# Encoder trunk: the first loads split into six transfers, x prepared by token tile, rstd ahead of the mask's cast, and branch B's mask added on VectorE in the row maximum

## The chip, the cores and the metric

One core of a Trainium2 chip runs the whole program. The metric is the time on the device in microseconds (us), lower is better. The kernel before took 861.21 us (median of 3 runs, 860.22 to 861.93). Engines are named as in the profile: PE (TensorE), DVE (VectorE), ACT (ScalarE), POOL (GpSimd), SP (SyncE).

## The reference

Two layers of an encoder on x of shape (1, 256, 1024), float32:

```
h  = rmsnorm(x);  z = h @ W_in            # columns: A q|k|v, B q|k|v, C pool, gates
A  = grouped-query attention, 8 heads, all 256 keys
B  = dilated windows, 3 groups x 4 slots: sc = where(valid, q.k / 8, -1e30)
     m = max(sc); p = exp(sc - m); groups joined by their softmax denominators
C  = centred mean pooling (windows 2/4/8/16) minus the token, a linear map
x += (sum_i sigmoid(gate_i) * P_i(branch_i)) @ W_out
x += SwiGLU(rmsnorm(x))
```

## The kernel before

All weights come as one stream of 136 units (68 for each layer) of 1 MB, each a tile of 128 partitions x 4 x 512 float32. SP loads them into a ring of four buffers, `w_raw` (L382 to L388); a buffer is loaded again when PE is done with its unit. Every float32 value is split into two float32r parts. ACT writes the high part (`w_hi`, L484, and for a layer's first unit in four quarters, L480), DVE subtracts to get the low part (`w_lo`, L621 and L627). The activations are split alike (`aT_hi` at L494, `aT_lo` at L654). PE then makes three matmuls of 512 columns for each product: hi x hi (L881), hi x lo (L883), lo x hi (L892). A unit has two token tiles m of 8 + 4 matmuls each.

The order is written by hand and is the same for all engines: for each unit t there is "before" work (`turns_before`), scores of attention pairs (units 11, 13, ..., 25), their transposes one unit later and the product with the values two units later, the unit's matmuls, and "within" work (`turns_within`). Each engine runs this list in order; semaphores tie them.

The start. `x_sb` holds x, tokens in two tiles. Half 0 of its columns (512 KB) is loaded by SP, half 1 by POOL. PE transposes four 128x128 blocks of it for each pair of half and tile (`("mix_x", i)`: i = 0, 1 are half 0 with tiles 0 and 1; i = 2, 3 are half 1), DVE multiplies by the norm's gain (L645), ACT makes the high part, DVE the low part. In unit 0, ACT splits the unit's four quarters, then units 1 and 2, and only then makes the high parts of mix_x 2 and 3; then it squares x with a sum (L530), and POOL makes rstd from the sums (L426, L420, L422). rstd is needed when ACT moves chunk z0 out of PSUM (L587, L588) in unit 1. POOL copies the identity and the mask to bfloat16 (L446, L448) before it makes rstd. DVE makes the rotary tables in unit 1 and from unit 2 on it rotates q and k (L693 to L717), between the low parts of the weights.

Attention. For each of 16 score tiles of 128x512 (two form a pair) PE writes scores to PSUM, DVE takes the row maximum with its sign changed (L731), ACT the exponential with a row sum (L516 to L523), DVE scales by the reciprocal of the sum (L742, L746), PE transposes (L914), ACT copies (L506). Tiles 8 to 15 are branch B. There the mask is added by PE: a bfloat16 matmul of the identity with the mask (L994) opens the accumulation and the scores (L1000) add to it.

Of the kernel before, what the change touches and what calls it, by code (L numbers as in the profile page):

```python
# [18 lines left out]
BF16 = mybir.dt.bfloat16  # L19
# [4 lines left out]
P = 128  # L24
# [3 lines left out]
NEG_INF = -1e30  # L28
MT = SEQ // P
KT = D // P  # L30
NC = 512
# [12 lines left out]
FIRST_BYTE, SMALL_BYTES = 4224, 11168  # L44
# [151 lines left out]
EARLY_TURNS = 2  # L196
BEFORE = -1
# [11 lines left out]
def build(nc, x, stream, params, b_gate, eye, angles, pooling, mask, out):  # L209
# [3 lines left out]
    with ExitStack() as ctx:  # L213
# [18 lines left out]
        mask_sb = sb("mask_sb", [P, P + MT * NC], BF16)  # L232
# [43 lines left out]
        ident_b = mask_sb[:, 0:P]  # L276
        mask_m = [mask_sb[:, P + m * NC:P + (m + 1) * NC] for m in range(MT)]
# [5 lines left out]
        x0_loaded = sem("x0_loaded")  # L283
# [5 lines left out]
        mask_ready = sem("mask_ready")  # L289
        gains_loaded = sem("gains_loaded")  # L290
        params_loaded = sem("params_loaded")
        bias_loaded = [sem(f"bias_loaded{i}") for i in range(2)]
        unit_landed = [sem(f"unit_landed{i}") for i in range(RING)]
        unit_done = sem("unit_done")
# [14 lines left out]
        max_ready = sem("max_ready")  # L309
        probs_ready = sem("probs_ready")  # L310
# [67 lines left out]
        @block.sync  # L378
        def _(sp):
            sp.dma_start(x_sb[:, :, 0:NC], xv[:, :, 0:NC]).then_inc(x0_loaded, 16)  # L380
            sp.dma_start(ident[:, :], eye).then_inc(eye_loaded, 16)
            with sp.Fori(0, DEPTH * UNITS // RING) as turn:  # L382
                for s in range(RING):

                    sp.wait_ge(unit_done, turn * RING + (s + 1))
                    sp.dma_start(w_raw[:, s, :, :].rearrange("p k n -> p (k n)"),  # L386
                                 stream_v[bass.ds((turn * RING + s) * P, P), :]
                                 ).then_inc(unit_landed[s], 16)  # L388

            ov = out.rearrange("b (p m) d -> (b p) m d", m=MT)  # L390
            for half, first in enumerate(X_BANKS):
                for m in range(MT):
                    sp.wait_ge(bank_free[first + m], DEPTH * USES[first + m] + 1)
                    cols = slice(NC * half, NC * half + NC)
                    sp.dma_start(ov[:, m, cols], x_sb[:, m, cols]).then_inc(out_done, 16)
            sp.wait_ge(out_done, 16 * 2 * MT)

        @block.gpsimd
        def _(pool):
# [9 lines left out]
            load_gains(0)  # L409
            pool.dma_start(x_sb[:, :, NC:D], xv[:, :, NC:D]).then_inc(x1_loaded, 16)  # L410
# [29 lines left out]
            for lay in range(DEPTH):  # L440
                load_bias(lay, 0)
                load_bias(lay, 1)
                if lay == 0:

                    pool.wait_ge(eye_loaded, 16)
                    nc.gpsimd.tensor_copy(mask_sb[:, 0:P], ident[:, :]).then_inc(mask_ready, 1)  # L446
                    pool.wait_ge(mask_loaded, 16)
                    nc.gpsimd.tensor_copy(mask_sb[:, P:], mask_f).then_inc(mask_ready, 1)  # L448
                x_norms(lay, 0, 0)
                if lay == 0:  # L450
                    pool.dma_start(pool_mat[:, :, :, :].rearrange("p m g n -> p (m g n)"), pooling
                                   ).then_inc(pooling_loaded, 16)
# [12 lines left out]
                x_norms(lay, 1, 2 + TURNED)  # L465

                wait_lo(pool, lay, ("ffn_x", 3))
                load_gains(min(lay + 1, DEPTH - 1))
                load_params(min(lay + 1, DEPTH - 1))

        @block.scalar
        def _(act):
            for b in range(0, 8):
                act.sem_inc(bank_free[b], 1)

            def split_first(lay):

                act.wait_ge(unit_landed[0], lay * (16 * UNITS // RING) + 16)
                for k in range(UK):
                    nc.scalar.activation(w_hi[:, 0, k, :], w_raw[:, 0, k, :], ACT.Copy).then_inc(first_hi, 1)  # L480
# [30 lines left out]
            def softmax_exp(lay, i):  # L511

                act.wait_ge(max_ready, lay * ATT + (i + 1))
                if i < 8:
                    m, h = i // 4, 4 * (i % 2) + 2 * (i // 2 % 2)
# [5 lines left out]
                else:  # L521
                    m, s = (i - 8) // 4, i % 4
                    last = nc.scalar.activation(probs[:, i % 2, :], B(("s", i))[:, :], ACT.Exp,  # L523
                                                bias=neg_max[:, 2 * i:2 * i + 1],
                                                accum_out=den[:, m, 8 + s:9 + s])
# [10 lines left out]
            act.wait_ge(x0_loaded, 16)  # L536
            for i in range(EARLY_TURNS):
                turn(BEFORE, ("mix_x", i))
            for lay in range(DEPTH):
                for t in range(UNITS):  # L540
                    for name in turns_before(t):
                        turn(lay, name)
                    if t == 0:
                        split_first(lay)
                    for j in splits_at(t, ahead=3):
                        split(lay, j)
# [11 lines left out]
                    for name in turns_within(t):  # L558
                        turn(lay, name)
# [9 lines left out]
                    if t % 2 == 1 and t // 2 <= POOL_CHUNK:  # L569
# [3 lines left out]
                        if c == 4:  # L573
                            act.wait_ge(mask_ready, 2)
# [31 lines left out]
        def _(dve):  # L606
# [121 lines left out]
            def row_max(lay, i):  # L728
                wait_full(dve, lay, ("s", i))
                k = 2 if i < 8 else 1  # L730
                nc.vector.tensor_reduce(neg_max[:, 2 * i:2 * i + k],  # L731
                                        B(("s", i))[:, :].rearrange("p (h n) -> p h n", h=k), AX_X, ALU.max,
                                        negate=True).then_inc(max_ready, 1)

            def norm_probs(lay, i):
# [5 lines left out]
                wait_emptied(dve, lay, ("s", i))  # L741
# [46 lines left out]
            dve.wait_ge(gains_loaded, 16)  # L788
            turns(BEFORE, [("mix_x", i) for i in range(EARLY_TURNS)])
            for lay in range(DEPTH):  # L790
# [3 lines left out]
                for t in range(UNITS):  # L794
# [4 lines left out]
                    if t == U_DOWN + 7:  # L799
                        dve.wait_ge(gains_loaded, lay * 16 + 32)  # L800
                    turns(lay, turns_before(t))
                    if t == 0:
                        split_first(lay)
                    if t in TURNS_FIRST:
                        turns(lay, turns_within(t))
# [60 lines left out]
        def _(pe):  # L866
            pe.sem_inc(unit_done, RING)

            def rows(lay, t, name, m, src, tiles, wk, first, final, opening=False):
# [4 lines left out]
                if first:  # L874
                    wait_free(pe, lay, (name, m))
                if opening and t:
# [21 lines left out]
            def columns(lay, t, name, src, tiles, first, final, wk=0):  # L898

                rows(lay, t, name, 0, src, tiles, wk, first, final, opening=wk == 0)  # L900
# [3 lines left out]
                return rows(lay, t, name, 1, src, tiles, wk, first, final)  # L904
# [66 lines left out]
            def scores(lay, p):  # L971
# [7 lines left out]
                if p == 4:  # L979
                    pe.wait_ge(mask_ready, 2)  # L980
# [11 lines left out]
                else:  # L992
                    for r in range(2):
                        nc.tensor.matmul(banks[r][:, :], ident_b, mask_m[m], start=True, stop=False)  # L994
                    for g in range(GROUPS):
# [3 lines left out]
                        for r in range(2):  # L999
                            last[r] = nc.tensor.matmul(banks[r][:, cols], qkT[rows_of[r], QT_B_Q + tile, tok],  # L1000
                                                       qkT[rows_of[r], QT_B_K + tile, keys], start=False,
                                                       stop=(g == GROUPS - 1))
# [29 lines left out]
            pe.wait_ge(x0_loaded, 16)  # L1032
            pe.wait_ge(eye_loaded, 16)
            for i in range(EARLY_TURNS):
                transposes(BEFORE, ("mix_x", i))
            for lay in range(DEPTH):
                for t in range(UNITS):
# [6 lines left out]
                    if t < U_C0:  # L1044
                        c, half = divmod(t, 2)
                        if c == 0:
                            for m in range(MT):
                                wait_lo(pe, lay, ("mix_x", 2 * half + m), former=half == 0)
                        last = columns(lay, t, f"z{c}", aT, range(UK * half, UK * half + UK), half == 0, half == 1)
# [15 lines left out]
                    elif t < U_FFN:  # L1065
                        half, n = divmod(t - U_OUT, 2)
                        if n == 0:
                            for m in range(MT):
                                wait_emptied(pe, lay, ("merged", 2 * half + m))
                        last = columns(lay, t, f"W{n}", aT, range(UK * half, UK * half + UK), half == 0, half == 1)  # L1070
                    elif t < U_DOWN:
                        i, half = divmod(t - U_FFN, 2)
                        if i == 0:
                            for m in range(MT):
                                wait_lo(pe, lay, ("ffn_x", 2 * half + m))
                        last = columns(lay, t, f"f{i}", aT, range(UK * half, UK * half + UK), half == 0, half == 1)
# [119 lines left out]
```

## Time and profile before

| what | value |
|---|---|
| the profiled execution's own time | 861.18 us |
| its span | 859.4 us |
| PE busy | 842.9 us, 98% |
| DVE busy | 552.0 us, 64% |
| ACT busy | 419.6 us, 49% |
| POOL busy | 74.1 us, 9% |

The span is what the profile covers; 1.8 us of the execution lie outside it. Busy shares are averages over stages. A pair of a time and a duration such as "11.69 0.77" is the start of a group of instructions and how long it lasted. "idle before" names how long the engine did nothing and what released it.

### The profile page before, as it was taken

Reading aid. Unit: us, or ns where it says so; the run is one execution under the profiler, and the core shown is the slowest. Engines: PE = TensorE matmul, PEld = TensorE weight load, DVE = VectorE, ACT = ScalarE, POOL = GpSimd, SP = SyncE. Lnnn points to the kernel's source line nnn. Section 1 sums busy time; section 2 is a strip of 40 time slices with the busy share of each in tenths; the row PEclk is TensorE's granted clock in tenths of the full one; section 3 lists DMA queues with packets and bytes.
Section 4 is the critical chain, followed back from the end, with each engine's and each line's share of the span. In section 5 each row is a group of like instructions: output and inputs, shape, how many; then the busy total and the mean of one; then the engine's idle time right before and its main releaser. Section 6 shows DMA issues by size and latency. Waiting matters only on the chain.

```text
span 859.4 us, 10421 instructions
## 1 busy us (share of the span) xinstructions
PE 842.9 (98%) x4060; PEld 687.1 (80%) x4068; DVE 552.0 (64%) x672; ACT 419.6 (49%) x505; POOL 74.1 (9%) x89
## 2 busy tenths in 40 slices
PE   4999999999999999999999999999999999999998
PEld 3788777878888888888888877878788888888886
DVE  3799556565876656564468985556576766566552
ACT  4665654455453444443446575443834544444340
POOL 2343000000002000000022420000000200000000
PEclk9999999999999999999999999999999999999999
DMA  8555434444547555555545543433454555555551
GB/s 327 210 183 195 147 117 154 172 147 148 191 153 240 195 176 174 189 196 195 180 170 194 191 153 142 170 131 141 148 196 170 193 195 186 170 185 192 196 184 61
DMA packets 22427, 151.59 MB, mean 176 GB/s; under 512 B 2624, under 2 KB 2800, under 8 KB 4848
## 3 DMA queue, kind: packets, MB, share of 16 engines
q1 hardware_dynamic: 20576, 144.25, 47.4%
q0 software_dynamic: 1808, 6.72, 2.3%
q8 instruction: 32, 0.52, 0.2%
q14 instruction: 11, 0.09, 0.0%
HBM read 149.91 MB, written 1.05 MB: 176 GB/s over the span
## 4 chain that ended last, share of the span: by engine, by line
PE 97%; DMA 2%; issue 0%; ACT 0%; SPq 0%; DVE 0%; ACTq 0%
PE bank L881 29%; PE bank L883 29%; PE bank L892 29%; PE bank L914 5%; PE bank L1025 2%; DMA w_raw<-in_stream_dram 2%; PE bank L1000 1%; PE bank L989 1%; PE bank L961 1%; PE bank L967 0%; PE bank L994 0%; ACT zvu L588 0%; DVE aT_lo L654 0%; ACT probsT L506 0%; SPq L386 0%
## 5 line engine op out<-in xcount | busy, mean ns | idle before, releaser
L621 DVE TENSOR_TENSOR w_lo<-w_raw,w_hi 128x2048 fp32r<-128x2048 f32 x134 | 306.3, 2288 | 130.9 <-ACT w_hi L484 130.6
L881 PE MATMUL bank<-w_hi,aT_hi 128*128 128x512 f32 x832 | 334.3, 402 | 6.8 <-ACT w_hi L480 4.9
L883 PE MATMUL bank<-w_hi,aT_lo 128*128 128x512 f32 x832 | 326.5, 392 | 0.0
L484 ACT ACTIVATE w_hi<-w_raw 128x2048 fp32r<-128x2048 f32 x134 | 256.3, 1913 | 106.1 <-DMA w_raw<-in_stream_dram 106.0
L892 PE MATMUL bank<-w_lo,aT_hi 128*128 128x512 f32 x832 | 224.2, 391 | 0.0
L881 PEld LDWEIGHTS bank<-w_hi,aT_hi 128*128 128x128 f32 x832 | 157.1, 189 | 43.4 <-issue 9.7
L892 PEld LDWEIGHTS bank<-w_lo,aT_hi 128*128 128x128 f32 x832 | 156.3, 188 | 33.2 <-DVE w_lo L627 0.2
L883 PEld LDWEIGHTS bank<-w_hi,aT_lo 128*128 128x128 f32 x832 | 157.3, 189 | 31.0
L881 PE MATMUL bank<-w_hi,hT_hi 128*128 128x512 f32 x176 | 68.9, 391 | 0.0
L883 PE MATMUL bank<-w_hi,hT_lo 128*128 128x512 f32 x176 | 68.5, 389 | 0.0
L499 ACT ACTIVATE hT_hi<-bank 128x512 fp32r<-128x512 f32 x22 | 13.2, 598 | 78.3 <-PE bank L914 78.3
L602 ACT ACTIVATE sg<-bank,rstd 128x256 f32<-128x256 f32 x44 | 20.9, 475 | 58.2 <-PE bank L892 51.8
L892 PE MATMUL bank<-w_lo,hT_hi 128*128 128x512 f32 x176 | 47.7, 389 | 0.0
L657 DVE TENSOR_TENSOR hT_lo<-bank,hT_hi 128x512 fp32r<-128x512 f32 x22 | 15.2, 692 | 41.1 <-ACT hT_hi L499 41.1
L731 DVE TENSOR_REDUCE neg_max<-bank 128x2 f32<-128x512 f32 (+1 forms) x32 | 20.6, 685 | 29.4 <-PE bank L1000 16.8
L506 ACT ACTIVATE probsT<-bank 128x512 f32<-128x512 f32 x32 | 17.5, 595 | 44.4 <-PE bank L914 44.2
L892 PEld LDWEIGHTS bank<-w_lo,hT_hi 128*128 128x128 f32 x176 | 33.0, 188 | 6.9
L881 PEld LDWEIGHTS bank<-w_hi,hT_hi 128*128 128x128 f32 x176 | 33.0, 188 | 6.8
L883 PEld LDWEIGHTS bank<-w_hi,hT_lo 128*128 128x128 f32 x176 | 33.1, 188 | 6.7
L426 POOL TENSOR_TENSOR sx<-ssx 128x2 f32<-128x2 f32 x4 | 4.3, 1080 | 361.5 <-ACT probsT L530 361.5
L850 DVE SCALAR_TENSOR_TENSOR scratch<-bank,rstd,sg 128x256 f32<-128x256 f32 x44 | 21.1, 481 | 21.2 <-ACT sg L602 21.2
L422 POOL TENSOR_TENSOR rs<-rs_in,neg_half 128x8 f32<-128x8 f32 (+2 forms) x24 | 32.8, 1365 | 2.0
(97 smaller groups left out, 704.0 us busy)
## 6 DMA issues: line engine op xcount, KB each, us to landing
w_raw<-in_stream_dram SPq DMA_DIRECT2D x136, 1024.0 KB, 4.7
bias_sb<-in_b_gate_dram POOLq DMA_DIRECT2D x12, 256.0 KB, 4.5
par<-in_params_dram POOLq DMA_DIRECT2D x3, 384.0 KB, 4.3
pool_mat<-in_pooling_dram POOLq DMA_DIRECT2D x1, 1024.0 KB, 8.3
out_dram<-x_sb SPq DMA_DIRECT2D x4, 256.0 KB, 4.0
x_sb<-in_x_dram SPq DMA_DIRECT2D x1, 512.0 KB, 3.7
x_sb<-in_x_dram POOLq DMA_DIRECT2D x1, 512.0 KB, 8.2
gates<-in_mask_dram POOLq DMA_DIRECT2D x1, 512.0 KB, 14.4
```

The lines of the kernel that those rows point to most:

```text
L422: nc.gpsimd.tensor_tensor(dst[0], dst[1], dst[2], ALU.pow).then_inc(signal, 1)
L484: nc.scalar.activation(w_hi[:, j % RING, :, :].rearrange("p k n -> p (k n)"), w_raw[:, j % RING, :, :].rearrange("p k n -> p (k n)"), ACT. ...
L506: free(nc.scalar.activation(probsT[:, i % 2, :], B(name)[:, :], ACT.Copy), name)
L602: nc.scalar.activation(sg[:, i % 2, m, :], B((f"f{i}", m))[:, 0:256], ACT.Sigmoid, scale=rstd[:, 1, m:m + 1]).then_inc(sig_done, 1)
L621: nc.vector.tensor_tensor(w[0], w[1], w[2].bitcast(F32), ALU.subtract).then_inc(unit_lo, 1)
L731: nc.vector.tensor_reduce(neg_max[:, 2 * i:2 * i + k], B(("s", i))[:, :].rearrange("p (h n) -> p h n", h=k), AX_X, ALU.max, negate=True).t ...
L850: made.append(link(nc.vector.scalar_tensor_tensor(scratch[:, 2 * NC + 256 * m:2 * NC + 256 * m + 256], B((f"f{i}", m))[:, 0:256], rstd[:, ...
L881: nc.tensor.matmul(o, src[0][:, k, tok], w_hi[:, slot, wk + i, :], start=first and i == 0, stop=False)
L883: nc.tensor.matmul(o, src[1][:, k, tok], w_hi[:, slot, wk + i, :], start=False, stop=False)
L892: last = nc.tensor.matmul(o, src[0][:, k, tok], w_lo[:, slot, wk + i, :], start=False, stop=final and i == len(tiles) - 1)
L914: return nc.tensor.transpose(b[:, at:at + P], src, ident[:, :])
L1025: last = nc.tensor.matmul(B(("o", o))[HD * r:HD * r + HD, at:at + w], zvu[:, kt, col(r):col(r) + HD], probsT[:, r, c:c + cw], start=(n == ...
```

## The change

- SP issues, before its loop: x half 0 tile 0, quarter 0 of unit 0, x half 0 tile 1, quarters 1 to 3 of unit 0 (six transfers of 256 KB), then x half 1 (512 KB, from POOL's queue to SP's), then units 1 to 3. The loop starts at the second turn.
- ACT issues the identity (from SP's queue) and the first layer's gains (from POOL's queue). POOL waits for x half 1 before it issues parameters, angles, mask and bias.
- PE runs 14 tiny matmuls on a constant tile once that tile is set, and 10 more after the transposes of mix_x 0 and 1.
- ACT and DVE prepare mix_x 1 after the quarters of unit 0; in layer 0 ACT makes the high parts of mix_x 2 and 3 ahead of the splits of units 1 and 2. PE waits for each token tile's low part by itself, also at W_out and the SwiGLU's first chunk.
- POOL makes rstd before it waits for the mask and casts it. There is no bfloat16 identity any more.
- Branch B: no mask matmuls. DVE's row maximum is one `tensor_tensor_reduce` that adds the mask, changes the sign, writes 128x512 to SBUF and keeps the row minimum; it frees the PSUM bank. ACT's exponential reads and writes that SBUF tile.

```diff
@@ SP
-            sp.dma_start(x_sb[:, :, 0:NC], xv[:, :, 0:NC]).then_inc(x0_loaded, 16)
-            sp.dma_start(ident[:, :], eye).then_inc(eye_loaded, 16)
-            with sp.Fori(0, DEPTH * UNITS // RING) as turn:
+            def first_piece(k):
+                sp.dma_start(w_raw[:, 0, k, :], stream_v[0:P, NC * k:NC * k + NC]).then_inc(piece_landed[k], 16)
+            sp.dma_start(x_sb[:, 0, 0:NC], xv[:, 0, 0:NC]).then_inc(x0_loaded[0], 16)
+            first_piece(0)
+            sp.dma_start(x_sb[:, 1, 0:NC], xv[:, 1, 0:NC]).then_inc(x0_loaded[1], 16)
+            for k in range(1, UK):
+                first_piece(k)
+            sp.sem_inc(unit_landed[0], 16)
+            sp.dma_start(x_sb[:, :, NC:D], xv[:, :, NC:D]).then_inc(x1_loaded, 16)
+            for s in range(1, RING):
+                sp.dma_start(w_raw[:, s, :, :].rearrange("p k n -> p (k n)"), stream_v[s * P:s * P + P, :]
+                             ).then_inc(unit_landed[s], 16)
+            with sp.Fori(1, DEPTH * UNITS // RING) as turn:
@@ POOL
-            load_gains(0)
-            pool.dma_start(x_sb[:, :, NC:D], xv[:, :, NC:D]).then_inc(x1_loaded, 16)
+            pool.wait_ge(x1_loaded, 16)
             load_params(0)
...
-                if lay == 0:
-                    pool.wait_ge(eye_loaded, 16)
-                    nc.gpsimd.tensor_copy(mask_sb[:, 0:P], ident[:, :]).then_inc(mask_ready, 1)
-                    pool.wait_ge(mask_loaded, 16)
-                    nc.gpsimd.tensor_copy(mask_sb[:, P:], mask_f).then_inc(mask_ready, 1)
                 x_norms(lay, 0, 0)
                 if lay == 0:
+                    pool.wait_ge(mask_loaded, 16)
+                    nc.gpsimd.tensor_copy(mask_sb[:, :], mask_f).then_inc(mask_ready, 1)
@@ ACT
+            act.dma_start(ident[:, :], eye).then_inc(eye_loaded, 16)
+            act.dma_start(par[:, 0:PR_GAIN], params_v[0:P, 0:PR_GAIN]).then_inc(first_gains, 16)
...
+                    wait_emptied(act, lay, ("s", i))
+                    nc.scalar.activation(probs[:, i % 2, :], probs[:, i % 2, :], ACT.Exp, scale=-1.0,
+                                         bias=neg_max[:, 2 * i:2 * i + 1],
+                                         accum_out=den[:, m, 8 + s:9 + s]).then_inc(exp_done, 1)
...
                     if t == 0:
                         split_first(lay)
+                        if lay == 0:
+                            turn(BEFORE, ("mix_x", 1))
+                            for name in turns_within(t):
+                                turn(lay, name)
                     for j in splits_at(t, ahead=3):
                         split(lay, j)
@@ DVE
+                    free(nc.vector.tensor_tensor_reduce(probs[:, i % 2, :], B(("s", i))[:, :], mask_m[(i - 8) // 4],
+                                                        -1.0, BIG, ALU.add, ALU.min, neg_max[:, 2 * i:2 * i + 1]),
+                         ("s", i))
...
-            turns(BEFORE, [("mix_x", i) for i in range(EARLY_TURNS)])
+            scale_turn(BEFORE, ("mix_x", 0))
+            scale_turn(BEFORE, ("mix_x", 1))
+            low_turn(BEFORE, ("mix_x", 0))
@@ PE
-                    for r in range(2):
-                        nc.tensor.matmul(banks[r][:, :], ident_b, mask_m[m], start=True, stop=False)
...
+            def warm_up(n):
+                for _ in range(n):
+                    nc.tensor.matmul(bank[WARM_BANK][0:MT * HEADS, 0:MT * HEADS],
+                                     neg_half[:, :, :].rearrange("p m h -> p (m h)"),
+                                     neg_half[:, :, :].rearrange("p m h -> p (m h)"), start=True, stop=True)
+            pe.wait_ge(half_ready, 1)
+            warm_up(WARM_LOADS)
             pe.wait_ge(eye_loaded, 16)
             for i in range(EARLY_TURNS):
+                pe.wait_ge(x0_loaded[i], 16)
                 transposes(BEFORE, ("mix_x", i))
+            warm_up(WARM_SPLITS)
```

## Rows read from the trace of the kernel before

**Rows 1.** The page's first part: busy time, share, instructions of each engine.
```profile
PE 842.9 (98%) x4060; PEld 687.1 (80%) x4068; DVE 552.0 (64%) x672; ACT 419.6 (49%) x505; POOL 74.1 (9%) x89
```
**Rows 2.** Waits of PE: who waited for whom, us in total, times, longest.
```profile
PE bank L881 <- ACT w_hi L480: 4.9, 1, 4.9
PE bank L881 <- DVE aT_lo L654: 1.9, 1, 1.9
```
**Rows 3.** Timeline of the first 30 us: start, duration, instructions merged, idle before.
```profile
4.85 1.94 PE L914 MATMUL bank<-ident,x_sb 128*128 128x128 f32 x8 [4.85 <-DMA ident<-in_eye_dram]
6.05 1.47 DVE L645 TENSOR_TENSOR scratch<-bank,par 128x512 f32<-128x512 f32 x2 [6.05 <-PE bank L914]
10.92 2.19 ACT L480 ACTIVATE w_hi<-w_raw 128x512 fp32r<-128x512 f32 x4 [2.74 <-DMA w_raw<-in_stream_dram]
14.73 1.91 ACT L484 ACTIVATE w_hi<-w_raw 128x2048 fp32r<-128x2048 f32 x1 [1.62 <-DMA w_raw<-in_stream_dram]
21.27 0.61 ACT L530 ACTIVATE probs<-x_sb 128x512 f32<-128x512 f32 x1
23.90 0.52 POOL L426 TENSOR_TENSOR sx<-ssx 128x2 f32<-128x2 f32 x1 [4.61 <-ACT probsT L530]
26.70 2.65 POOL L422 TENSOR_TENSOR rstd<-sx,neg_half 128x2 f32<-128x2 f32 x1
28.52 1.07 PE L892 MATMUL bank<-w_lo,aT_hi 128*128 128x512 f32 x4
```
**Rows 4.** DMA issues of the first 12 us: KB each, median us to landing.
```profile
x_sb<-in_x_dram SPq DMA_DIRECT2D x1, 512.0 KB, 3.7
gates<-in_mask_dram POOLq DMA_DIRECT2D x1, 512.0 KB, 14.4
```
**Rows 5.** Two windows: busy us of PE, PEld, DVE, ACT, POOL, PE's clock, DMA share, GB/s.
```profile
23.08:26.49 3.41, 3.41 (x10) 2.66 (x9) 3.41 (x3) 2.53 (x5) 2.50 (x2) 0.52 0.48 199
40.20:88.10 47.90, 47.78 (x224) 38.70 (x222) 47.15 (x77) 30.85 (x47) 16.48 (x20) 1.00 0.50 176
```
**Rows 6.** Timeline rows of DVE and PE, 33 to 89 us.
```profile
33.65 2.29 DVE L621 TENSOR_TENSOR w_lo<-w_raw,w_hi 128x2048 fp32r<-128x2048 f32 x1 [2.99 <-ACT w_hi L484]
...
40.20 2.29 DVE L621 TENSOR_TENSOR w_lo<-w_raw,w_hi 128x2048 fp32r<-128x2048 f32 x1 [1.54 <-ACT w_hi L484]
...
86.43 1.07 PE L892 MATMUL bank<-w_lo,aT_hi 128*128 128x512 f32 x4
...
87.57 0.62 DVE L746 TENSOR_SCALAR probs<-probs,rden 128x256 f32<-128x256 f32 x2
...
88.31 0.42 PEld L914 LDWEIGHTS bank<-ident,probs 128*128 128x128 f32 x4 [0.31 <-issue]
```
**Rows 7.** PE's timeline where the scores of branch A, then branch B, begin.
```profile
79.22 1.08 PE L892 MATMUL bank<-w_lo,aT_hi 128*128 128x512 f32 x4
...
80.22 1.14 PE L989 MATMUL bank<-qkT 64*128 64x256 f32 x8
...
157.11 1.08 PE L892 MATMUL bank<-w_lo,aT_hi 128*128 128x512 f32 x4
...
158.56 1.15 PE L1000 MATMUL bank<-qkT 64*128 64x256 f32 x12
```
**Rows 8.** DVE's operations by line, then timeline rows of pair 5.
```profile
L731 DVE TENSOR_REDUCE neg_max<-bank 128x2 f32<-128x512 f32 (+1 forms) x32 | 20.6, 685 | 29.4 <-PE bank L1000 16.8
L621 DVE TENSOR_TENSOR w_lo<-w_raw,w_hi 128x2048 fp32r<-128x2048 f32 x134 | 306.3, 2288 | 130.9 <-ACT w_hi L484 130.6
...
L833 DVE SCALAR_TENSOR_TENSOR gates<-bank,rstd,bias_sb x24: 739/748/751, 116.5 to 615.6; 128x512 f32<-128x512 f32 x24
...
163.93 0.49 DVE L746 TENSOR_SCALAR probs<-probs,rden 128x512 f32<-128x512 f32 x1
...
166.06 1.02 PEld L914 LDWEIGHTS bank<-ident,probs 128*128 128x128 f32 x8
```

More of the change, by code:

```diff
@@ L27 @@
 EPS = 1e-6
-NEG_INF = -1e30
+NEG_INF, BIG = -1e30, 3e38
 MT = SEQ // P
@@ L293, in build @@
         unit_landed = [sem(f"unit_landed{i}") for i in range(RING)]
+        piece_landed = [sem(f"piece_landed{k}") for k in range(UK)]
         unit_done = sem("unit_done")
@@ L535, in _ @@
             nc.scalar.activation(table_warm[:, :], neg_half[:, 0, 0:MT], ACT.Exp)
-            act.wait_ge(x0_loaded, 16)
-            for i in range(EARLY_TURNS):
-                turn(BEFORE, ("mix_x", i))
+            for m in range(MT):
+                act.wait_ge(x0_loaded[m], 16)
+            turn(BEFORE, ("mix_x", 0))
             for lay in range(DEPTH):
@@ L867, in _, with rows @@
             pe.sem_inc(unit_done, RING)
-            def rows(lay, t, name, m, src, tiles, wk, first, final, opening=False):
+            def rows(lay, t, name, m, src, tiles, wk, first, final, opening=False, ready=None):
                 tok = slice(P * m, P * m + P)
@@ L896, in rows, with columns @@
                 return last
-            def columns(lay, t, name, src, tiles, first, final, wk=0):
-                rows(lay, t, name, 0, src, tiles, wk, first, final, opening=wk == 0)
+            def columns(lay, t, name, src, tiles, first, final, wk=0, ready=None):
+                rows(lay, t, name, 0, src, tiles, wk, first, final, wk == 0, ready)
                 if wk == 0 and t not in TURNS_FIRST:
@@ L903, in columns @@
                         transposes(lay, turn)
-                return rows(lay, t, name, 1, src, tiles, wk, first, final)
+                return rows(lay, t, name, 1, src, tiles, wk, first, final, False, ready)
             def transposes(lay, name):
@@ L1045, in _ @@
                         c, half = divmod(t, 2)
[L1046 to L1049, printed above, removed]
+                        ready = (lambda m: wait_lo(pe, lay, ("mix_x", 2 * half + m), former=half == 0)) if c == 0 else None
+                        last = columns(lay, t, f"z{c}", aT, range(UK * half, UK * half + UK), half == 0, half == 1,
+                                       ready=ready)
                     elif t in (U_C0, U_C1):
@@ L1066, in _ @@
                         half, n = divmod(t - U_OUT, 2)
[L1067 to L1070, printed above, removed]
+                        ready = (lambda m: wait_emptied(pe, lay, ("merged", 2 * half + m))) if n == 0 else None
+                        last = columns(lay, t, f"W{n}", aT, range(UK * half, UK * half + UK), half == 0, half == 1,
+                                       ready=ready)
                     elif t < U_DOWN:
                         i, half = divmod(t - U_FFN, 2)
[L1073 to L1076, printed above, removed]
+                        ready = (lambda m: wait_lo(pe, lay, ("ffn_x", 2 * half + m))) if i == 0 else None
+                        last = columns(lay, t, f"f{i}", aT, range(UK * half, UK * half + UK), half == 0, half == 1,
+                                       ready=ready)
                     else:
```

57 lines of the change are left out of this document (33 added, 24 removed).

## The prediction

> **What bounds the kernel now.** I read the page's busy shares first. PE is busy 842.9 of 859.4 us [rows 1], so only PE's idle time, its work and its clock can be worth anything. PE's waits come next: beside the first loads they hold one wait of 4.9 us before its first matmul of unit 0 and one of 1.9 us before unit 1 [rows 2]. Together with the first transposes at 4.85 us [rows 3] all of the idle time lies in the first 23 us. The timeline of that stretch shows who is late: ACT's split of unit 0 waits for the DMA until 10.92, its split of unit 1 until 14.73 [rows 3]. PE ends unit 1 at 28.52 + 4 x 0.227 = 29.43 us (0.227 us is the pitch of these matmuls: four take 1.07, which is three pitches and one duration of 0.39). That 29.43 is my reference point at the start.
>
> Then I looked at windows for an engine that is full beside PE. From 40.20 to 88.10 us DVE is busy 47.15 of 47.90 us [rows 5]: rotations between weight splits. At its end PE has its last matmul of unit 11 at 86.43 (done at 87.34), DVE normalizes the first pair's probabilities at 87.57 (done 88.1), and PE's second group of their weight loads starts at 88.31, right behind [rows 6]. So in layer 0 PE and DVE reach unit 12 together, and PE already waits about 0.3 us there. Whoever starts PE earlier must start DVE earlier too.
>
> **The change part by part.**
>
> *First loads.* x's half 0 (512 KB) landed 3.7 us after its issue at 0.73 [rows 4], at 4.4. Half of it first in the queue lands at about 3.8 (256 KB at about 400 GB/s is 0.65 us). Tile 1 is third, 512 KB behind, so about 5.2; the quarters follow 0.65 us apart up to 7.2, x half 1 at 8.6, unit 1 at 11.3, unit 2 at 14 to 15, unit 3 at 17 to 19, since POOL's loads join at about 10. I take 4.1 for the identity, which PE had to wait for until 4.85 [rows 3] as second in SP's queue.
>
> *First matmul.* PE transposes tile 0 at 4.1 and tile 1 at 5.2 (8 took 1.94, so 4 take 0.9 to 1.0); the first scaling started 1.2 us behind the transposes' start and takes 0.73 [rows 3], so DVE scales tile 0 at 5.3 and tile 1 at 6.4 to 7.1, and makes the low part of tile 0 by 7.8. ACT has quarter 0 ready by 7.1, and all four by 8.8 (0.55 each, rows 3). The first matmul is at 7.8 instead of 11.69 = 3.9 us earlier. The 14 tiny matmuls lie before 4.1 and the 10 before 7.8: I cost them at nothing; if each took 0.2 us the ten would end at 8.0 and cost 0.2.
>
> *Unit 0 and 1.* DVE makes the four low quarters by 10.4, the low part of tile 1 by 11.1, then scales mix_x 2 and 3; ACT's high parts of them are done by 13.1 if PE runs unit 0 at the high clock, by 14.5 if at the low one. ACT splits unit 1 by 15.1 (1.91 us, rows 3), DVE's low part is there at 17.3, PE ends unit 1 at about 20.9 (16 hi matmuls, two short waits). PE would be 8.5 us ahead; with the low clock in unit 0, 7.1 us. The 1.9 us wait [rows 2] is inside this, its cause (ACT made mix_x 2 and 3 behind the split of unit 2) is gone.
>
> *rstd.* ACT: split of unit 1 to 15.1, unit 2 to 17.0, squares from 17.1; squares to POOL's first step took 23.90 - 21.27 = 2.6 us, POOL's three steps 26.70 + 2.65 - 23.90 = 5.45 us [rows 3]. rstd is ready at 25.2 instead of 29.35: 4.15 us earlier, less than PE's 8.5. The mask's cast is 1 us on POOL that did not stand in the way before (POOL waited 4.61 us for the squares, rows 3), so its move is worth 0; but POOL now meets the mask's wait behind rstd. The mask took 14.4 us to land [rows 4]; issued at about 10 it is there by 24.4, before rstd: 0. In the worst case, with all of POOL's loads 5 us later, POOL's first head norms (needed 7 us behind rstd) still don't wait.
>
> *DVE.* Its split of unit 4 began 33.65 - 29.35 = 4.3 us behind rstd, since ACT moves z0 first; it idled 1.54 us before the split of unit 5 [rows 6], whose load ran beside the 1 MB pooling matrix. Now unit 5's load starts at about 21, well ahead of that matrix: this idle time should go. DVE reaches the first pair's probabilities 4.15 + 1.54 = 5.7 us earlier, at 82.4 instead of 88.1. Bounds: 4.15 (idle time stays) less 1.3 (low clock in unit 0, late landing) = 2.9, and 8.8 (no gate: 8.5 and the 0.3 of waiting). I take 5.7, since the stretch behind it is full work.
>
> *PE at unit 12.* PE is ready at 87.34 - 8.5 = 78.8 and DVE at 81.7 for the first tile: a new wait of about 2.9 us (1.5 with the low clock in unit 0). After the one wait of this size (1.9 us) the granted clock stood at 0.52, the lower level of 1.2 GHz, from 23.08 to 26.49 [rows 5], costing half of 3.41 = 1.7 us. I count that again here.
>
> *Mask matmuls.* From the last low matmuls' start to the scores' start branch B has 158.56 - 157.11 = 1.45 us, branch A 80.22 - 79.22 = 1.00 us [rows 7]. 0.45 us for each of 4 pairs in 2 layers: 3.6 us of PE's time, all on the path.
>
> *The new row maximum.* The trace has no such operation. Nearest rows: a reduction from PSUM of the same shape 0.685 us, a three-operand op from PSUM 0.748, and, far off, 2.29 for four times the elements [rows 8]. I take 0.75, with ends 0.68 and 2.29. Pair 5 shows the room: DVE is done at 163.93 + 0.49 = 164.42, PE reads at 166.06 [rows 8], 1.64 us of slack, and two such operations at 0.75 take 0.13 more than now. Even double passes (1.37 each) stay inside. The exponential now reads SBUF; ACT is idle half of the time. So 0. The Trainium skill ("VectorE: DVE Perf Modes", section on two Vector instructions with no wait between them) says that an operation with an accumulator output is two instructions. No row of DVE here shows a second one; by that rule both tiles of a pair get a bit longer, inside the slack.
>
> The Trainium skill ("DMA: Bandwidth & Descriptors", rules for kernel authors) holds that spreading DMAs over engines brings no bandwidth, as all share the same 16 DMA engines. By it moving loads between SP, ACT and POOL is worth only what their order is worth, and that is how I cost them.
>
> *PE's waits by token tile* at W_out and the SwiGLU: PE has no wait there now (none in rows 2), so 0.
>
> Sum, against the profiled execution: 861.2 (861.18, span 859.4; the median is 861.21, so nothing to correct) - 5.7 + 1.7 - 3.6 = 853.6 us.
>
> **The rivals.**
>
> *The clock stays up at unit 12.* The wait may be split in two by the first tile's transposes, or shorter. For it: 1.5 us if PE is slower in unit 0. Against it: the only precedent fell. Time: 853.6 - 1.7 = 851.9.
>
> *DVE is no gate.* DVE's lag behind PE would have to be made up. For it: ACT and the loads run ahead, PE's lead is real. Against it: 47.15 of 47.90. Time: 861.2 - 8.8 - 3.6 = 848.8.
>
> *The start is later than I think.* 256 KB transfers of 2 KB rows, POOL's loads in front of unit 2, PE at the low clock in unit 0: rstd moves by only 2.9 us. With a short wait at unit 12 that keeps the clock, or a long one: 861.2 - 2.9 - 3.6 (+ 1.7) = 854.7 to 856.4.
>
> *Slower.* The new DVE operation is slow, as when it makes several passes over a PSUM source. Each pair then holds PE by 2(x - 0.685) - 1.64 = 2x - 3.0 us, eight times. It decides at 7.6 = 8(2x - 3.0), x = 1.98 us. At 2.29 [rows 8] it gives 8 x 1.6 = 12.6 us: 866.2. For it: the operation is not in the trace. Against it: both near rows lie at 0.7.
>
> *The change does not do what it says.* PE's first data could be held by something that I don't see, for instance ACT's issue of DMAs before its table load; then only the mask's 3.6 us are left with part of the start, 857.
>
> **How the numbers follow.** Forecast 0.43 (853.6); clock stays 0.25 (851.9); later start 0.15 (855.5); no gate 0.08 (848.8); little at the start 0.04 (857.3); slower 0.05 (866). A measurement of this kernel tells 0.2%, 1.7 us, from no change. Faster: all but the last and a little of the one before, 0.94; same 0.02; slower 0.04. The range leaves out "no gate", the slow case and some of the edges: 850.3 to 857.0.
>
> **What would show it.** First L881 matmul at about 7.8 us; rstd's L422 ends near 25; the 1.9 us wait for aT_lo is gone; DVE full from about 34 to 82; a PE wait of 1.5 to 3 us at L914 near 79 to 82 us, followed by a stretch of clock 0.5; L1000 starts 1.00 us after the last L892 row; the new DVE operation near 0.75 us and no wait of PE for probabilities of branch B. I am wrong if PE passes unit 12 without a wait, if the new operation is over 1.5 us, or if unit 2 starts later than 24 us.

## The result and the profile after

The changed kernel takes 849.45 us (median of 4 runs, 848.44 to 850.21) beside 861.43 us of the kernel before in the same comparison: ratio 0.9865 (95% interval 0.9851 to 0.988), 10.3 to 12.8 us less. I had forecast 853.6 us with a range of 850.3 to 857.0. The direction was right, the size wrong: the start gave about twice what I had put down for it.

The spans of the two profiled executions differ by 859.4 - 847.9 = 11.5 us. First the page's busy shares and PE's waits (us in total, times, longest) of the changed kernel:

```profile
PE 842.3 (99%) x4100; PEld 689.4 (81%) x4100; DVE 552.7 (65%) x688; ACT 420.1 (50%) x505; POOL 69.2 (8%) x86
```
```profile
PE bank L1067 <- POOL neg_half L422: 0.9, 1, 0.9
PE bank L950 <- ACT probsT L521: 0.8, 2, 0.4
PE bank L950 <- DMA ident<-in_eye_dram: 0.3, 1, 0.3
PE bank L950 <- DMA x_sb<-in_x_dram: 0.2, 1, 0.2
```

Both waits of [rows 2] are gone, and no new one of any size has come; PE's 5.9 us of tiny matmuls (L1067; each of the 24 stands as two records, so x28 and x20 below) count as busy here, so the busy time hardly falls although 3.6 us of mask work are gone.

The timeline of the start (line numbers have moved: L667 was L645, L495 was L480, L917 was L881, L928 was L892, L547 was L530, L439, L433 and L435 were L426, L420 and L422):

```profile
4.64 1.12 PE L950 MATMUL bank<-ident,x_sb 128*128 128x128 f32 x4 [0.26 <-DMA ident<-in_eye_dram]
5.92 1.12 PE L950 MATMUL bank<-ident,x_sb 128*128 128x128 f32 x4 [0.16 <-DMA x_sb<-in_x_dram]
...
6.82 2.48 PE L1067 MATMUL bank<-neg_half 128*68 128x68 f32 x20
...
7.21 2.18 ACT L495 ACTIVATE w_hi<-w_raw 128x512 fp32r<-128x512 f32 x4
...
9.05 0.77 PE L917 MATMUL bank<-w_hi,aT_hi 128*128 128x512 f32 x1
...
17.74 0.61 ACT L547 ACTIVATE probs<-x_sb 128x512 f32<-128x512 f32 x1
...
20.37 0.25 POOL L439 TENSOR_TENSOR sx<-ssx 128x2 f32<-128x2 f32 x1 [7.34 <-ACT probsT L547]
...
20.71 0.19 POOL L433 TENSOR_SCALAR sx<-sx 128x2 f32<-128x2 f32 x1
...
20.98 0.72 POOL L435 TENSOR_TENSOR rstd<-sx,neg_half 128x2 f32<-128x2 f32 x1
...
21.27 1.07 PE L928 MATMUL bank<-w_lo,aT_hi 128*128 128x512 f32 x4
```

PE ends unit 1 at 21.27 + 0.91 = 22.18, against 28.52 + 0.91 [rows 3]: 7.25 us earlier. rstd is ready at 21.70 instead of 29.35: 7.65 us earlier. Of this POOL's own three steps make 4.1: they take 1.33 us from 20.37, and took 5.45 us [rows 3]. DVE's weight subtractions beside them, first in the kernel before (where they run from 22.09 to 28.78), then in the changed kernel, which has a gap from 20.57 to 22.12:

```profile
22.09 6.69 DVE L621 TENSOR_TENSOR w_lo<-w_raw,w_hi 128x2048 fp32r<-128x2048 f32 x3
```
```profile
16.07 4.50 DVE L643 TENSOR_TENSOR w_lo<-w_raw,w_hi 128x2048 fp32r<-128x2048 f32 x2 [1.11 <-ACT w_hi L499]
22.12 2.73 DVE L643 TENSOR_TENSOR w_lo<-w_raw,w_hi 128x2048 fp32r<-128x2048 f32 x1 [1.56 <-ACT w_hi L499]
```

DVE and PE up to unit 12, from DVE's timeline and PE's (L643 was L621, L776 was L746):

```profile
26.67 2.28 DVE L643 TENSOR_TENSOR w_lo<-w_raw,w_hi 128x2048 fp32r<-128x2048 f32 x1
...
31.68 2.29 DVE L643 TENSOR_TENSOR w_lo<-w_raw,w_hi 128x2048 fp32r<-128x2048 f32 x1
...
79.41 0.61 DVE L776 TENSOR_SCALAR probs<-probs,rden 128x256 f32<-128x256 f32 x2
```
```profile
79.14 1.07 PE L928 MATMUL bank<-w_lo,aT_hi 128*128 128x512 f32 x4
...
79.83 1.02 PEld L950 LDWEIGHTS bank<-ident,probs 128*128 128x128 f32 x8
```

DVE's split of unit 4 is 6.98 us earlier than in [rows 6], that of unit 5 8.52, the first pair's probabilities 8.16 (79.41 against 87.57). The split of unit 4 gained less than rstd because something else became the last to be ready: ACT has its high part at 26.41, but DVE is busy from 22.12 to 26.67 with the split of unit 3 and its rotary tables. PE is 7.29 us earlier at its last matmuls of unit 11 (79.14 against 86.43) and then loads all eight blocks of probabilities in one go from 79.83, where [rows 6] have a second group at 88.31. So PE gains 7.9 us up to here: 7.3 and the 0.6 that it lost at this place. The other 3.6 are the mask matmuls:

```profile
133.76 1.07 PE L928 MATMUL bank<-w_lo,aT_hi 128*128 128x512 f32 x4
134.76 0.95 PEld L1033 LDWEIGHTS bank<-qkT 64*128 64x128 f32 x12 [0.35 <-issue]
```

Scores of branch B now begin 1.00 us behind the last low matmuls' start, as in branch A; before it was 1.45 [rows 7]. 8 x 0.45 = 3.6, and 7.9 + 3.6 = 11.5.

The changed kernel was profiled a second time (e10 below), and its first 10 us differ. There the ten tiny matmuls took 1.39 us instead of 2.48, and PE had the pitch of the high clock from the first matmul on. Its rows of the tiny matmuls, of the first matmul and of the starts of units 2 and 12:

```profile
6.54 1.39 PE L1067 MATMUL bank<-neg_half 128*68 128x68 f32 x20
8.13 0.47 PE L917 MATMUL bank<-w_hi,aT_hi 128*128 128x512 f32 x1 [0.20 <-issue]
...
20.85 0.39 PE L917 MATMUL bank<-w_hi,aT_hi 128*128 128x512 f32 x1
...
79.92 0.47 PE L917 MATMUL bank<-w_hi,aT_hi 128*128 128x512 f32 x1
```

e2, e3, e4, e7 and e8, which make the same 24 tiny matmuls, have 1.39 or 1.40 us there too, so the execution read above is the odd one. In e10 PE ends unit 1 8.58 us earlier than before (20.85 against 29.43) and is 8.8 us earlier behind unit 12's transposes (79.92 against 88.72), where it lost some 0.4 us to DVE. Its span is 847.0 us.

The new DVE operation, by its line (duration in ns: least, median, most):

```profile
L758 DVE CUSTOM_DVE_ANT_0 probs<-bank,mask_sb x16: 685/688/692, 135.9 to 598.0; 128x512 f32<-128x512 f32 x16
L758 DVE DVE_READ_ACCUMULATOR2_ANT neg_max<- x16: 81/82/84, 136.6 to 598.6; 128x1 f32 x16
```

### The profile page after: what moved, and what is told of

Same layout as the page of the kernel before. It is cut to its first block, busy times and chain, and to the rows that moved or that the text cites. A ratio compares the mean times of both kernels' runs of the same rounds, so it can differ in the third digit from the quotient of the medians.

```text
span 847.9 us, 10500 instructions
## 1 busy us (share of the span) xinstructions
PE 842.3 (99%) x4100; PEld 689.4 (81%) x4100; DVE 552.7 (65%) x688; ACT 420.1 (50%) x505; POOL 69.2 (8%) x86
## 4 chain that ended last, share of the span: by engine, by line
PE 98%; ACT 1%; DMA 0%; DVE 0%; SPq 0%; issue 0%
PE bank L917 30%; PE bank L919 29%; PE bank L928 29%; PE bank L950 5%; PE bank L1057 2%; PE bank L1033 1%; PE bank L1024 1%; PE bank L997 1%; DMA x_sb<-in_x_dram 0%; PE bank L1003 0%; DVE w_lo L643 0%; PE bank L1067 0%; ACT w_hi L499 0%; ACT zvu L610 0%; ACT aT_hi L509 0%; ACT probsT L521 0%
## 5 line engine op out<-in xcount | busy, mean ns | idle before, releaser
L643 DVE TENSOR_TENSOR w_lo<-w_raw,w_hi 128x2048 fp32r<-128x2048 f32 x134 | 307.0, 2293 | 128.3 <-ACT w_hi L499 128.0
L917 PE MATMUL bank<-w_hi,aT_hi 128*128 128x512 f32 x832 | 333.3, 401 | 0.0
L928 PE MATMUL bank<-w_lo,aT_hi 128*128 128x512 f32 x832 | 223.7, 391 | 0.1
L917 PEld LDWEIGHTS bank<-w_hi,aT_hi 128*128 128x128 f32 x832 | 156.6, 188 | 36.0 <-issue 5.0
L928 PEld LDWEIGHTS bank<-w_lo,aT_hi 128*128 128x128 f32 x832 | 155.6, 188 | 33.4 <-DVE w_lo L643 0.6
L917 PE MATMUL bank<-w_hi,hT_hi 128*128 128x512 f32 x176 | 68.9, 391 | 0.0
L928 PE MATMUL bank<-w_lo,hT_hi 128*128 128x512 f32 x176 | 47.7, 389 | 0.0
L679 DVE TENSOR_TENSOR hT_lo<-bank,hT_hi 128x512 fp32r<-128x512 f32 x22 | 15.2, 692 | 40.8 <-ACT hT_hi L514 40.8
L928 PEld LDWEIGHTS bank<-w_lo,hT_hi 128*128 128x128 f32 x176 | 33.0, 188 | 6.9
L917 PEld LDWEIGHTS bank<-w_hi,hT_hi 128*128 128x128 f32 x176 | 33.0, 188 | 6.7
L439 POOL TENSOR_TENSOR sx<-ssx 128x2 f32<-128x2 f32 x4 | 4.0, 1010 | 362.4 <-ACT probsT L547 362.4
L435 POOL TENSOR_TENSOR rs<-rs_in,neg_half 128x8 f32<-128x8 f32 (+2 forms) x24 | 33.2, 1381 | 2.0
L816 DVE TENSOR_TENSOR x_sb<-bank,x_sb 128x512 f32<-128x512 f32 x16 | 10.6, 686 | 28.6 <-PE bank L928 28.6
```

Source lines behind the costliest of these rows:

```text
L435: nc.gpsimd.tensor_tensor(dst[0], dst[1], dst[2], ALU.pow).then_inc(signal, 1)
L643: nc.vector.tensor_tensor(w[0], w[1], w[2].bitcast(F32), ALU.subtract).then_inc(unit_lo, 1)
L679: ins = nc.vector.tensor_tensor(turn_dest(name, False), turn_view(name, B(name)[:, :]), hi, ALU.subtract)
L917: nc.tensor.matmul(o, src[0][:, k, tok], w_hi[:, slot, wk + i, :], start=first and i == 0, stop=False)
L928: last = nc.tensor.matmul(o, src[0][:, k, tok], w_lo[:, slot, wk + i, :], start=False, stop=final and i == len(tiles) - 1)
```

## Experiments

Theory P: POOL's small steps for rstd took 5.45 us before because they had to wait for DVE's 128x2048 subtractions that ran beside them; in the changed kernel they meet the gap in DVE's work. Rival O: their length came from what POOL did before (DMA issues, the mask's cast). Beside these, gate theory: in layer 0 DVE's chain decides when PE gets past unit 12.

**One half of the change each.** e1 is the kernel before with branch B's part alone, e2 the changed kernel with branch B's part taken back. In short (arguments left out, and with them the exponential, its semaphore and, in e2, the bfloat16 identity that POOL copies again behind rstd):

```diff
 e1, on the kernel before                      e2, on the changed kernel
-  matmul(banks[r], ident_b, mask_m[m])        +  matmul(banks[r], ident_b, mask_m[m])
-  tensor_reduce(... max, negate=True)         -  tensor_tensor_reduce(... add, min)
+  tensor_tensor_reduce(... add, min)          +  tensor_reduce(... max, negate=True)
```

> The kernel before with only branch B's part of the change: no mask matmuls on PE, the mask added by DVE in the row maximum, the exponential in place. My theory (mask matmuls are worth 0.45 us for each of 8 pairs, the DVE work is hidden): 861.4 - 3.6 = 857.8 us. Rival (part of the gain after unit 12 came from here, or the new DVE operation holds PE): 859.5 or more, or below 856.5.

> The changed kernel with the mask back on PE (identity and mask in bfloat16, row maximum and exponential as before): only the start is changed. Theory read from the two traces (PE reaches unit 12 at 80.85 instead of 88.72): 861.4 - 7.9 = 853.5 us. Rival, the sum that I forecast for the start (-5.7 + 1.7): 857.4.

e1: 856.76 us, ratio 0.9953 (0.994 to 0.9967), that is 2.8 to 5.2 us less than 860.17. e2: 851.97 us, ratio 0.9907 (0.9891 to 0.9923), 6.6 to 9.4 us less. The mask's 3.6 us hold; the start's -4.0 as I had summed it lies outside e2's interval, 7.9 inside. The halves add up (ratios 0.0047 and 0.0093 below 1, the whole 0.0135).

**DVE busy while POOL makes rstd.** e3 makes the subtraction for unit 2 twice; e4 is the same edit with `j == 3`.

```diff
+                if lay == 0 and j == 2:
+                    nc.vector.tensor_tensor(qkT[:, 0:8, :].rearrange("p k n -> p (k n)"), w[1], w[2].bitcast(F32),
+                                            ALU.subtract).then_inc(extra, 1)
+                    dve.wait_ge(extra, 1)
```

> The changed kernel, in which DVE makes the subtraction for unit 2 of layer 0 twice (once more into a tile that is free then), so that DVE is in a 128x2048 subtraction while POOL makes rstd. Theory P (POOL's three small steps are stretched because they wait for DVE's long subtractions; 5.45 us before against 1.33 after): the steps take 3.5 to 5.4 us, rstd is ready at 24 to 26 instead of 21.7, DVE reaches the first pair's probabilities 2.5 to 4 us later, PE waits 2 to 3.5 us at unit 12: 852 to 855 us, the upper part if the clock falls behind that wait. Rival O (the steps' length comes from what POOL did just before, its DMA issues or the mask's cast): the steps stay at 1.3 us, DVE only 0.5 us later: 850 us.

> As the run with unit 2 twice, but for unit 3, behind rstd. rstd should stay at 21.7 us and DVE be 2.2 us later from unit 4's subtraction on. Theory (DVE is full up to unit 12 and just level with PE there, 79.94 against 80.06): PE waits about 2.1 us at the first pair's transposes; 851.6 us if the clock stays up, 853.3 us if it falls behind the wait as it did behind the wait of 1.9 us in the kernel before. Rival (DVE has room before unit 12): 849.5.

e3: 851.74 us, ratio 0.9892 (0.9875 to 0.9908); e4: 851.11 us, 0.9889 (0.9871 to 0.9906). By the ratios both are some 2 us slower than the changed kernel (0.9865), but the intervals overlap at their ends (its own goes to 0.988), so the times alone do not settle it; the traces are clearer. The profiled execution of e3 is the slowest of its five (849.85 to 852.96). POOL and DVE in e3, then PE's largest wait and the window behind it (busy us of PE, PEld, DVE, ACT, POOL, then PE's clock, DMA share, GB/s):

```profile
19.53 2.17 POOL L440 TENSOR_TENSOR sx<-ssx 128x2 f32<-128x2 f32 x1 [6.71 <-ACT probsT L548]
21.79 2.11 POOL L434 TENSOR_SCALAR sx<-sx 128x2 f32<-128x2 f32 x1
23.98 0.79 POOL L436 TENSOR_TENSOR rstd<-sx,neg_half 128x2 f32<-128x2 f32 x1
```
```profile
17.03 2.29 DVE L645 TENSOR_TENSOR qkT<-w_raw,w_hi 128x2048 f32<-128x2048 f32 x1
19.36 4.49 DVE L648 TENSOR_TENSOR w_lo<-w_raw,w_hi 128x2048 fp32r<-128x2048 f32 x2
```
```profile
PE bank L955 <- DVE probs L781: 2.6, 1, 2.6
```
```profile
82.50:86.50 4.00, 4.00 (x14) 3.14 (x13) 2.67 (x6) 2.56 (x3) 1.55 (x2) 0.57 0.15 61
```

POOL's steps take 5.24 us (19.53 to 24.77). The first two, 0.25 and 0.19 us long in the changed kernel, end at 21.70 and 23.90, each within 0.1 us of the end of one of DVE's subtractions (about 21.6 and 23.85); the third, next to DVE's short table operations, takes 0.79. POOL had done nothing different before them: O falls, P holds. The rest is what I had forecast for the changed kernel itself: PE waits 2.6 us at unit 12, and behind it the granted clock is 0.57, the level of 1.2 GHz for most of 4 us. Against e10, whose first 10 us are alike, PE's last matmuls of unit 11 come at the same time (77.74 against 77.85) and the first pair's probabilities 2.6 us later (81.36 against 78.77): the wait is DVE's delay.

In e4 rstd's steps stay at 0.19, 0.19 and 0.72 us, as P says, and DVE is later all the same: split of unit 4 at 28.91. PE waits for DVE at unit 12:

```profile
PE bank L955 <- DVE probs L781: 1.4, 1, 1.4
```
```profile
82.30:86.00 3.70, 3.70 (x21) 3.12 (x20) 2.36 (x6) 2.79 (x4) 1.55 (x2) 1.00 0.49 206
```

So DVE is a gate for PE there, only the changed kernel's DVE was early enough to meet PE. The wait is shorter than the 2.1 us that I expected, since PE was late itself: in this execution it had waited 1.8 us for x's tile 1, against 0.6 in e10. Behind the wait of 1.4 us the clock stayed at 1.00.

**The tiny matmuls.** e5: `WARM_LOADS, WARM_SPLITS = 1, 0, 0` behind the bank number; e6: `14, 4`.

> The changed kernel without any of the 24 tiny matmuls. In the changed kernel PE's first matmul (9.05) starts when the ten behind the transposes end, 0.7 us after the low part of tile 0 is ready, and the matmuls are at the low clock until about 10.5. Theory (the tiny matmuls bring the clock up early): the first matmul is at 8.4, but the low clock lasts 4 us as in the kernel before (11.69 to 15.9), PE ends unit 0 about 1 us later, ACT and DVE too: 850.5 us. Rival (they bring nothing but their own length): 848.8.

> The changed kernel with 4 tiny matmuls behind the transposes instead of 10 (14 before them stay). If the clock rises at the same time: first matmul at 8.4 instead of 9.05, everything behind up to unit 1 0.6 us earlier, 848.8 us, too little to be told from 849.4 by time, so the trace is to show it. If the ten are needed for the clock: low clock beyond 11 us and no gain or a loss of 0.5.

e5: 850.08 us, 0.9883 (0.9868 to 0.9898). e6: 850.23 us, 0.9883 (0.9868 to 0.9898). The times tell neither from the changed kernel. In e5's trace all eight first matmuls come 0.43 us apart (8.41 to 11.54), the low level, though the profile's granted clock reads 1.00 there, and unit 2 begins at 22.45. In e6 the first matmul is at 8.27, with 0.23 us from one to the next at once, and unit 2 begins at 20.99. Beside the execution read at the top (22.18) four tiny matmuls look 1.2 us better than ten, but beside e10 (20.85) they bring nothing: what differs is the clock of the first 10 us, and two executions of one kernel differ in it. Against e10, leaving out all 24 costs 1.6 us at unit 2 and 1.1 us of the span (848.1 against 847.0). That is one trace each, and the medians do not tell it.

**POOL's order.** e7 puts the cast back ahead of rstd:

```diff
+                if lay == 0:
+                    pool.wait_ge(mask_loaded, 16)
+                    nc.gpsimd.tensor_copy(mask_sb[:, :], mask_f).then_inc(mask_ready, 1)
                 x_norms(lay, 0, 0)
                 if lay == 0:
-                    pool.wait_ge(mask_loaded, 16)
-                    nc.gpsimd.tensor_copy(mask_sb[:, :], mask_f).then_inc(mask_ready, 1)
```

> The changed kernel with the mask's wait and cast back ahead of rstd on POOL (the order of before). My forecast costed this step at 0. Theory P (POOL's small steps are stretched by DVE's long subtractions): the mask lands at 20 to 22 us, the cast takes 1 to 3 us, and the steps then fall into DVE's subtraction for unit 3 instead of its idle time: rstd at 24.5 to 26.5 instead of 21.7, a wait of PE of 1.5 to 3 us at unit 12, 851.5 to 854 us. Rival (steps of 1.3 us whatever DVE does): rstd at 23.5, 850 us or less.

851.99 us, 0.9892 (0.9873 to 0.991). POOL in e7:

```profile
21.96 2.46 POOL L459 CAST mask_sb<-gates 128x1024 bf16<-128x1024 f32 x1 [9.21 <-DMA gates<-in_mask_dram]
24.49 0.18 POOL L439 TENSOR_TENSOR sx<-ssx 128x2 f32<-128x2 f32 x1
...
25.04 0.77 POOL L435 TENSOR_TENSOR rstd<-sx,neg_half 128x2 f32<-128x2 f32 x1
```

rstd at 25.8, PE waits 2.5 us at unit 12 again, with a granted clock of 0.54 behind it (83.7 to 87.0). It is not the steps that grew (they met DVE's short table operations) but the mask, which landed at 22 us, and its cast beside a subtraction, 2.46 us instead of 1.03. My expectation had the right time for a partly wrong reason. The trace also speaks against O: the cast came right before the steps, and they stayed short. The five runs lie far apart (849.6, 849.7, 851.99, 853.43, 853.93, the last one profiled), and the interval overlaps that of the changed kernel: in the median the step that I had costed at 0 is worth about 2 us once rstd is early, in two runs of five nothing can be seen of it.

**ACT's order.** e8 takes it back in the changed kernel, e9 puts it alone into the kernel before:

The part of each edit that moves the call (the guard at its old place is left out):

```diff
 e8, on the changed kernel                     e9, on the kernel before
                 split_first(lay)                              split_first(lay)
                 if lay == 0:                  +               if lay == 0:
                     turn(BEFORE, ("mix_x", 1))
-                    for name in turns_within(t):  +               for name in turns_within(t):
-                        turn(lay, name)           +                   turn(lay, name)
```

> The changed kernel, but ACT makes the high parts of mix_x 2 and 3 behind the splits of units 1 and 2, as before. The wait of PE before unit 1 should come back with about 3.5 us (ACT done with unit 2 at 18, the high parts at 19, DVE's low parts at 19.7, instead of a start of unit 1 at 16.2), and the clock falls behind it (1.7 us): 854.5 us. Rival (DVE is level with PE at unit 12, and its chain starts at rstd, so a delay of PE alone is partly hidden there): 851 to 852.

> The kernel before with one thing of the change: in layer 0 ACT makes the high parts of mix_x 2 and 3 ahead of the splits of units 1 and 2. Theory: PE's wait of 1.9 us before unit 1 goes and with it the stretch of low clock behind it, and POOL's three steps for rstd fall into a time in which DVE waits for ACT's split of unit 3, so that they take 1.3 instead of 5.4 us: rstd at about 26 instead of 29.35, PE starts unit 2 about 3 us earlier and keeps that past unit 12: 857.2 us against 860.2. Rival (the steps stay at 5.4 us and DVE's chain holds PE at unit 12): 859.5, with a wait of PE at unit 12.

e8: 853.05 us, 0.9918 (0.9905 to 0.9932), some 4.5 us slower than the changed kernel by the ratios, between the theory's time and the rival's. PE waits 3.5 us before unit 1, the clock behind it (18.30 to 21.80) is 0.52, and POOL's steps are back to the lengths of the kernel before, step by step, since they now lie beside DVE's three subtractions (18.79 to 25.48):

```profile
20.61 0.53 POOL L439 TENSOR_TENSOR sx<-ssx 128x2 f32<-128x2 f32 x1 [7.76 <-ACT probsT L547]
21.22 2.11 POOL L433 TENSOR_SCALAR sx<-sx 128x2 f32<-128x2 f32 x1
23.41 2.65 POOL L435 TENSOR_TENSOR rstd<-sx,neg_half 128x2 f32<-128x2 f32 x1
```

PE is so late by its own wait that it passes unit 12 without one. So e8's time says little on rstd; its trace shows the steps' length.

e9: 858.11 us against 859.81, ratio 0.9972 (0.9963 to 0.9981), 1.6 to 3.2 us less. The profiled execution's first weights landed 1.35 us late (ACT's first quarter at 12.27 instead of 10.92, rows 3), yet rstd is ready 2 us earlier than before:

```profile
26.04 0.25 POOL L426 TENSOR_TENSOR sx<-ssx 128x2 f32<-128x2 f32 x1 [6.35 <-ACT probsT L530]
26.38 0.19 POOL L420 TENSOR_SCALAR sx<-sx 128x2 f32<-128x2 f32 x1
26.65 0.72 POOL L422 TENSOR_TENSOR rstd<-sx,neg_half 128x2 f32<-128x2 f32 x1
```
```profile
21.73 4.49 DVE L625 TENSOR_TENSOR w_lo<-w_raw,w_hi 128x2048 fp32r<-128x2048 f32 x2 [0.91 <-ACT w_hi L484]
25.86 1.90 ACT L484 ACTIVATE w_hi<-w_raw 128x2048 fp32r<-128x2048 f32 x1
27.79 2.29 DVE L625 TENSOR_TENSOR w_lo<-w_raw,w_hi 128x2048 fp32r<-128x2048 f32 x1 [1.56 <-ACT w_hi L484]
```

This is the kernel before with its own POOL code; only ACT's order differs, and 5.45 us have become 1.33. In both orders ACT splits unit 3 behind the squares. But before, DVE held back the subtractions of units 1 and 2 until ACT had made the high parts of mix_x 2 and 3, and ran all three in one go; here it has ended the first two at 26.22 and has nothing to subtract until 27.79, while POOL works. PE has no wait at unit 12. The time does not separate the two effects of the order (PE's 1.9 us wait before unit 1 is gone too), and it lies between the theory's 857.2 and the rival's 859.5.

**A version beyond.** e11: four tiny matmuls, and DVE scales the first pair ahead of the split:

```diff
+                    if p == 0:
+                        norm_probs(lay, 0)
+                        norm_probs(lay, 1)
                     for j in splits_at(t):
                         split(lay, j)
-                    if p is not None:
+                    if p:
```

> The changed kernel once more, as the comparison for the run with four tiny matmuls and early probabilities on the same chip: about 1.35% below the kernel before.

> The changed kernel with 4 instead of 10 tiny matmuls behind the transposes, and with DVE scaling the first pair's probabilities ahead of the weight split of unit 13, in both layers. In the changed kernel PE's second load of probabilities in layer 1 still waits for DVE (497.67), about 0.5 us. If both count: 0.6 + 0.5 = 1.1 us less than the changed kernel, 848.3 us. If DVE's reordering only delays its split of unit 13, the same time as the changed kernel, 849.4.

e10, the changed kernel again: 848.72 us, 0.9871 (0.9855 to 0.9886). e11: 848.47 us, 0.9874 (0.9855 to 0.9893). No difference that can be told; in this execution of e11 PE waited 0.9 us for a low part of x in unit 0 instead.

## Why the prediction was wrong

- **What bounds.** Right: PE, and in layer 0 DVE just beside it at unit 12 (the first point where PE needs the softmax's result). e3, e4 and e7 show the gate by PE waits of 2.6, 1.4 and 2.5 us there.
- **First loads and first matmul.** Forecast 7.8, measured 9.05, and 8.13 in e10. The identity and x's tile 1 came 0.5 and 0.7 us later than I had them (4.64 and 5.92), so the low part of tile 0 was ready at 8.35. The ten tiny matmuls, which I had costed at nothing or 0.2, took 0.25 us each in this execution (6.82 to 9.30) and held PE for another 0.7 us; in e10 they took 0.14 each and held nothing.
- **Unit 0 and 1.** Forecast PE 8.5 us ahead, or 7.1 with the low clock in unit 0; measured 7.25 with the low pitch up to 10.5, and 8.58 in e10. Both figures of that step held.
- **rstd: the step that failed.** I had taken "POOL's three steps 5.45 us" from [rows 3] as a fixed duration and moved it. It was a wait in disguise: beside the steps DVE's subtractions ran without a gap up to 28.78, 0.57 us before the last step's end. My own working had DVE idle from the split of unit 2 on, with ACT at the squares, so the gap could have been seen. ACT and the squares were 0.65 us late, POOL's steps 4.1 us shorter, rstd at 21.7 instead of 25.2. e3 (5.24 us with a subtraction put back), e8 (5.29 us of busy steps, 5.45 from end to end) and e9 (1.33 us in the kernel before) show the cause.
- **DVE.** The 1.54 us of idle time before unit 5 did go (6.98 became 8.52). Full work up to unit 12: right, so of rstd's 3.5 us 2.5 came through to its end: 79.9 instead of 82.4. 0.7 went at the split of unit 4, where DVE's own work was the last to be ready, and 0.4 behind unit 5.
- **PE at unit 12 and the clock.** The wait of 2.9 us and the 1.7 us of low clock did not come; PE and DVE met within 0.2 us. In e10, with PE's lead of 8.6, DVE was there 8.8 us earlier than before (78.77 against 87.57), and PE lost some 0.4 us. The rival that DVE is no gate gave 848.8 and came nearest, but that is luck: DVE is a gate that had moved as far as PE. The cost of the gate was sized well, as e3 shows (2.6 us, then the low level for nearly 4 us).
- **Moving the cast.** I costed it at 0 with rstd at 25.2. With rstd at 21.7 the mask's landing at 22 is in the way, and e7 puts some 2 us on it in the median, with runs from 0 to 4: an error that follows from the first.
- **Mask matmuls.** 3.6 forecast, 3.6 in the trace, e1's interval 2.8 to 5.2.
- **New row maximum.** 0.75 forecast, 0.688 and 0.082 for reading the accumulator measured, together 0.77, no wait of PE for it. By the Trainium skill's rule of two instructions ("VectorE: DVE Perf Modes") the trace agrees: there is a second one.

The sum in the terms of the forecast: start -7.9 (-8.8 in e10) instead of -5.7 + 1.7, mask -3.6 as forecast.

## What to carry to other kernels

A duration of a small operation on POOL is only a duration if DVE was not in a long one beside it: compare the ends of both, and where they fall together, take the length from another place of the trace. When a step is moved, ask what its neighbours on the other engines will be doing at its new place. And two engines that are level at one point both have to be moved: reckon each one's lead by itself, and mistrust a difference of 3 us that rests on one number. Before a microsecond at a kernel's start is put down to an edit, read a second execution of the same kernel: here two differed by 1.3 us at unit 2.

## What the runs showed of the hardware

- Adding two columns on POOL takes 0.19 to 0.25 us, or 2.17 us (e3) when it meets a 128x2048 float32 subtraction with both inputs in SBUF on DVE; it ends when that ends, and the profile shows the whole of it as busy. It works the other way too: with POOL's cast of the mask beside it DVE's subtraction in the changed kernel took 2.73 us instead of 2.29, and in e4 cast and subtraction held each other in turn, the cast 3.06 us instead of 1.03, the next subtraction 3.01:

```profile
21.89 3.06 POOL L461 CAST mask_sb<-gates 128x1024 bf16<-128x1024 f32 x1 [0.60 <-DMA gates<-in_mask_dram]
24.09 3.01 DVE L648 TENSOR_TENSOR w_lo<-w_raw,w_hi 128x2048 fp32r<-128x2048 f32 x1
```

The Trainium skill states it ("SBUF — State Buffer", section on who interferes with whom): DVE with two SBUF inputs and a POOL operation that reads SBUF share a port pair under an exclusive lock, and the second to start waits for the whole of the first. The traces agree to within 0.2 us, and I had not looked it up for a step that I only moved.
- TensorE's clock: behind waits of 1.9 us (kernel before), 2.5 (e7), 2.6 (e3) and 3.5 (e8) the granted clock fell to the level of 1.2 GHz for a few us (0.52 to 0.57). Behind one of 1.4 us (e4) it did not, nor was the pitch of the low level seen behind e4's 1.8 us before the transposes of tile 1. That is six cases and no rule. In a first stretch the granted clock can read 1.00 while matmuls come 0.43 us apart (e5, 8.4 to 11.9; the kernel before, 11.69 to 15.2).
- The mask, a 512 KB load, landed between 20 and 23 us in the runs of the changed start (POOL's cast waited for it until 22.27 in e10 and 23.17 in e11), so a wait that looks free in one execution is not in another.
